# Squares among the gate groups, V's products on two engines and the scan in two halves

## What is computed

```python
h = rms_norm(x, ab_norm_g[i])
proj = h @ ab_w_in[i]
u, q, k, v, gate, a_logit, b_logit = jnp.split(proj, split_points, axis=-1)
a_out = s5_mixer(u, ...)          # 32 groups of 16 channels, 64 complex states
b_out = gated_deltanet(q, k, v, gate, a_logit, b_logit, ...)   # 4 heads, 8 chunks of 64
x = x + jnp.concatenate([a_out, b_out], axis=-1) @ ab_w_out[i]
...
# s5_mixer: s_t = lam_bar * s_(t-1) + b_bar u_t ; y = real(c s_t) + d*u_t ; gelu, then gated
# gated_deltanet: q, k, v through a 4-tap convolution and silu
q = l2_norm(heads(q)) * (GDN_HEAD_DIM ** -0.5)
k = l2_norm(heads(k))
lower = jnp.eye(CHUNK, dtype=F32) + beta[..., :, None] * kk * decay_strict
sol = lax.linalg.triangular_solve(lower, rhs, left_side=True, lower=True, unit_diagonal=True)
```

## Time and profile before

| | us |
|---|---|
| median of 3 runs | 1708.27 (1707.21 to 1708.54) |
| profiled execution, its own time | 1708.71 |
| span of its trace | 1706.9 |
| PE busy | 1648.6 |
| DVE busy | 768.2 |
| ACT busy | 623.9 |
| POOL busy | 253.4 |

### The profile page before, as it was taken

The page is one execution under the profiler, slowest core; times in us unless marked ns, Lnnn a source line. Parts: engine busy times, 40 slices in busy tenths (PEclk is TensorE's granted clock), DMA queues, the critical chain, the costliest instruction groups (busy, mean ns, idle before and its releaser), DMA issues.

```text
span 1706.9 us, 22635 instructions
## 1 busy us (share of the span) xinstructions
PE 1648.6 (97%) x9358; PEld 1343.3 (79%) x9358; DVE 768.2 (45%) x1006; ACT 623.9 (37%) x1010; POOL 253.4 (15%) x315
## 2 busy tenths in 40 slices
PE   5989989999999999999999999999999999999999
PEld 4778788788878788888888887567887788888887
DVE  4658435555444444443225435773453444444222
ACT  6533433344434322221114336564452522222110
POOL 3863034010000211110000003110000011111000
PEclk9999899999999999999999999999999999999999
DMA  6610212034212333332223332322212243333221
GB/s 203 135 50 1 75 52 71 31 123 149 74 49 75 99 98 98 96 97 88 92 95 99 99 123 99 96 78 99 80 45 74 60 113 98 93 93 94 91 98 74
DMA packets 146801, 151.85 MB, mean 89 GB/s; under 512 B 8864, under 2 KB 109344, under 8 KB 146592
## 3 DMA queue, kind: packets, MB, share of 16 engines
q1 hardware_dynamic: 146720, 150.69, 28.9%
HBM read 147.53 MB, written 3.15 MB: 88 GB/s over the span
## 4 chain that ended last, share of the span: by engine, by line
PE 88%; DVE 6%; ACT 4%; issue 2%; POOL 0%; DMA 0%; SPq 0%; DVEq 0%; ACTq 0%; POOLq 0%
PE ps L329 24%; PE ps L331 24%; PE ps L330 24%; PE ps L2070 1%; PE ps L1730 1%; PE ps L425 1%; PE ps L2100 1%; DVE sb L610 1%; PE ps L1707 1%; PE ps L964 1%; DVE w_lo_ab L301 1%; PE ps L2088 1%; ACT sb L1741 1%; ACT sb L2159 1%; PE ps L1242 1%
## 5 line engine op out<-in xcount | busy, mean ns | idle before, releaser
L329 PE MATMUL ps<-h_hi,w_hi 128*128 128x512 f32 x864 | 338.7, 392 | 4.4 <-DVE w_lo L1904 3.9
L330 PE MATMUL ps<-h_lo,w_hi 128*128 128x512 f32 x864 | 337.2, 390 | 0.0
L301 DVE TENSOR_TENSOR w_lo<-raw,w_hi 128x2048 fp32r<-128x2048 f32 x66 | 155.0, 2349 | 341.7 <-ACT w_hi L297 341.7
L297 ACT ACTIVATE w_hi<-raw 128x2048 fp32r<-128x2048 f32 x84 | 160.8, 1915 | 377.1 <-PE ps L331 376.4
L331 PE MATMUL ps<-h_hi,w_lo 128*128 128x512 f32 x704 | 274.4, 390 | 0.0
L329 PEld LDWEIGHTS ps<-h_hi,w_hi 128*128 128x128 f32 x864 | 162.9, 189 | 39.2 <-issue 4.7
L330 PEld LDWEIGHTS ps<-h_lo,w_hi 128*128 128x128 f32 x864 | 162.9, 189 | 33.5
L1904 DVE TENSOR_TENSOR w_lo<-raw,w_hi 128x2048 fp32r<-128x2048 f32 x44 | 138.1, 3139 | 53.5 <-ACT w_hi L1886 53.5
L331 PEld LDWEIGHTS ps<-h_hi,w_lo 128*128 128x128 f32 x704 | 132.5, 188 | 27.8
L1886 ACT ACTIVATE w_hi<-raw 128x2048 fp32r<-128x2048 f32 x44 | 84.3, 1916 | 161.2 <-PE ps L331 161.2
L1914 POOL CAST a_hi<-up 128x512 f32 x44 | 27.0, 613 | 777.2 <-DVE up L1902 777.2
(11 more groups left out here) (378 smaller groups left out, 2697.3 us busy)
## 6 DMA issues: line engine op xcount, KB each, us to landing
raw<-in_f_w_gate SPq DMA_DIRECT2D x44, 512.0 KB, 4.0
raw<-in_f_w_up SPq DMA_DIRECT2D x44, 512.0 KB, 5.2
raw<-in_f_w_down SPq DMA_DIRECT2D x44, 512.0 KB, 4.2
raw<-in_xa_w_kv SPq DMA_DIRECT2D x16, 1024.0 KB, 5.0
raw<-in_c_w_qkv SPq DMA_DIRECT2D x12, 1024.0 KB, 5.1
raw<-in_ab_w_in SPq DMA_DIRECT2D x10, 1024.0 KB, 6.0
raw<-in_xa_w_q SPq DMA_DIRECT2D x8, 1024.0 KB, 5.0
raw<-in_xa_w_out SPq DMA_DIRECT2D x8, 1024.0 KB, 5.0
```

The source lines that it names most:

```text
L297: a.activation(w_hi[:, n % 2, :], raw[n % 2], ACT.Copy).then_inc(sem("w_hi"), 1)
L301: v.tensor_tensor(w_lo(n)[:, n % 2, :], raw[n % 2], w_hi[:, n % 2, :].bitcast(F32), ALU.subtract).then_inc(sem("w_lo"), 1)
L329: pe.matmul(out, a[0], b[0], start=start, stop=False)
L330: pe.matmul(out, a[0], b[1], start=False, stop=False)
```

## The change

Seven things change, all in the first mixer. (1) V's real block goes to GpSimd and its imaginary block to VectorE, each with a scratch of its own. GpSimd's waits only for the tables and for u's copy in DRAM, and lies over u; so u is read back from DRAM (`s5_u_back_sp`, 1 MB) into the place of the output sum. (2) On ScalarE the tables' copies go ahead of silu 7, and TM's copies ahead of piece 8, convolution 9 and silu 8. (3) On VectorE the padded C goes ahead of piece 7 and convolution 7. (4) The 8 squares are put among groups 18 and 19. (5) The scan is done in two halves of 8 group pairs; its banks are arranged so that half 0 frees banks 4 and 5, and `s5_out_pe` works half by half. (6) GpSimd makes the first level's mask of a tile right behind its U_m, and `solve_pe` turns each tile when its own U_m is there. (7) On the last tile ScalarE does the exponential before the copy of q.

```diff
-        V_re, V_im = reg(arena, S5_GP, 8, S5_CH), reg(arena + 2048, S5_GP, 8, S5_CH)
-        v_tmp = reg(base + 10240, S5_GP, 8, S5_CH)
+        V_re, V_im = reg(base + 2048, S5_GP, 8, S5_CH), reg(arena, S5_GP, 8, S5_CH)
+        v_tmp = [reg(base + 10240, S5_GP, 8, S5_CH), reg(arena + 2048, S5_GP, 8, S5_CH)]
...
+                    if k == 4 and mid is not None:
+                        mid()
...
             if f == 0:
-                a.wait_ge(sem("s5_v"), 1)
+                a.wait_ge(sem("s5_vre"), 1)
...
-            g.wait_ge(sem("s5_x"), 2)
+            g.wait_ge(sem("u_out"), 16)
+            g.wait_ge(sem("s5_tab"), 10)
             cr, ci, vr, vi = s5_v_operands()
-            link(g, g.tensor_tensor(V_im, cr, vi, ALU.mult), ch)
-            g.wait_ge(sem("s5_vre"), 1)
-            link(g, g.tensor_tensor(v_tmp, ci, vr, ALU.mult), ch)
-            link(g, g.tensor_tensor(V_im, V_im, v_tmp, ALU.add), "s5_v")
+            link(g, g.tensor_tensor(V_re, cr, vr, ALU.mult), ch)
+            link(g, g.tensor_tensor(v_tmp[0], ci, vi, ALU.mult), ch)
+            link(g, g.tensor_tensor(V_re, V_re, v_tmp[0], ALU.subtract), "s5_vre")
...
+        def s5_u_back_sp(sp):
+            sp.wait_ge(panel_used, AB_PIECES)
+            sp.dma_start(yP, u_dram.rearrange("(f g) c n -> (g c) f n", f=4)).then_inc(sem("u_back"), 16)
...
+            for half in range(2):
+                X_re, X_im = (ps[:, 4 + 2 * half + ri, :].rearrange("p (g c) -> p g c", c=S5_C) for ri in range(2))
+                a, b, c, er, ei, r8 = (w[:, 8 * half:8 * half + 8] for w in (t_a, t_b, t_c, E_re, E_im, R8))
+                link(v, v.tensor_tensor(a, X_re, er, ALU.mult), ch)
...
+                v.memset(a[:, :, 0:1], 0.0).then_inc(sem("s5_carry"), 1)
...
+            for half in range(2):
+                pe.wait_ge(sem("s5_carry"), half + 1)
+                for gp in range(8 * half, 8 * half + 8):
+                    direct(S5_GP + gp)
+                for gp in range(8 * half, 8 * half + 8):
...
         def s5_glu_dve(v):
+            v.wait_ge(sem("u_back"), 16)
...
+                g.wait_ge(sem("g_u"), i + 1)
+                g.tensor_tensor(A_l[:, i], A_T[:, i], bc(ccol("m2"), 1, GH), ALU.mult).then_inc(sem("sv_mask"), 1)
...
         def solve_pe(pe):
-            pe.wait_ge(sem("g_at"), TT)
+            pe.wait_ge(sem("g_tok"), 3 * TT)
             for i in range(TT):
-                pe.wait_ge(sem("g_u"), TT)
+                if i == TT - 1:
+                    pe.wait_ge(sem("g_at"), TT)
+                pe.wait_ge(sem("g_u"), i + 1)
...
-            ab_groups_pe(pe, 15, 19)
-            gdn_squares_pe(pe)
+            ab_groups_pe(pe, 15, 17)
+            gdn_squares_pe(pe, 0, 2)
+            ab_groups_pe(pe, 18, 18, mid=lambda: gdn_squares_pe(pe, 2, 3))
+            gdn_squares_pe(pe, 3, 5)
+            ab_groups_pe(pe, 19, 19, mid=lambda: gdn_squares_pe(pe, 5, 6))
+            gdn_squares_pe(pe, 6, 2 * GH)
...
             for n in range(12):
+                if n == 9:
+                    s5_tm_act(a)
                 if n % 2:
                     pieces_hi(a, *ab_ahead(n + 4))
                 conv_act(a, n)
+                if n == 8:
+                    s5_tables_act(a)
                 if n >= 1:
                     silu_act(a, n - 1)
-                if n == 8:
-                    s5_tables_act(a)
-                if n == 9:
-                    s5_tm_act(a)
...
-            for f in range(4):
-                gate_act(a, f)
-            gdn_squares_act(a, 2, 2 * GH)
+            gate_act(a, 0)
+            gate_act(a, 1)
+            gdn_squares_act(a, 2, 5)
+            gate_act(a, 2)
+            gdn_squares_act(a, 5, 2 * GH)
+            gate_act(a, 3)
...
-                gdn_back_act(a, i)
-                gdn_dec_act(a, i)
...
+                else:
+                    gdn_dec_act(a, i)
+                    gdn_back_act(a, i)
```

More of the change, by code:

```diff
@@ L570, in ab_wait, with ab_groups_pe @@
                 eng.wait_ge(panel_used, where[f"ab{m // 4}_{m % 4 // 2}"] + 1)
-        def ab_groups_pe(pe, first, last):
+        def ab_groups_pe(pe, first, last, mid=None):
             for m in range(first, last + 1):
@@ L754, in s5_v_dve @@
             cr, ci, vr, vi = s5_v_operands()
-            link(v, v.tensor_tensor(V_re, cr, vr, ALU.mult), "dve_step")
-            link(v, v.tensor_tensor(v_tmp, ci, vi, ALU.mult), "dve_step")
-            v.tensor_tensor(V_re, V_re, v_tmp, ALU.subtract).then_inc(sem("s5_vre"), 1)
+            link(v, v.tensor_tensor(V_im, cr, vi, ALU.mult), "dve_step")
+            link(v, v.tensor_tensor(v_tmp[1], ci, vr, ALU.mult), "dve_step")
+            v.tensor_tensor(V_im, V_im, v_tmp[1], ALU.add).then_inc(sem("s5_v"), 1)
         def s5_pad_dve(v):
@@ L887, in s5_out_pe, with direct @@
             pe.wait_ge(sem("gate_s"), 4)
-            for n in (*range(4, S5_GP), *range(4), *range(S5_GP, S5_G)):
+            def direct(n):
                 gp, g2, o = place(n)
+                pe.matmul(o, U2[:, 2 * gp + g2, :], TM[:, 2 * gp + g2, :], start=(gp % 4 == 0), stop=False, skip_group_check=True)
+            for n in (*range(4, S5_GP), *range(4)):
                 if n == 0:
                     pe.wait_ge(sem("g_roots"), after("g_roots", 1))
-                if n == S5_GP:
-                    pe.wait_ge(sem("s5_carry"), 1)
-                pe.matmul(o, U2[:, 2 * gp + g2, :], TM[:, 2 * gp + g2, :], start=(gp % 4 == 0), stop=False, skip_group_check=True)
@@ L895, in s5_out_pe @@
-            pe.wait_ge(sem("s5_carry"), 1)
+                direct(n)
             pe.wait_ge(sem("s5_v"), 1)
[L897 to L907, removed]
+            for half in range(2):
[3 more added lines that the diff above has]
+                for gp in range(8 * half, 8 * half + 8):
+                    for g2 in range(2):
+                        _, _, o = place(gp + S5_GP * g2)
+                        r = slice(g2 * 64, g2 * 64 + 64)
+                        pe.matmul(o, t_b[r, gp, :], V_re[r, gp, :, :].rearrange("p i c -> p (i c)"), start=False, stop=False, skip_group_check=True)
+                    for g2 in range(2):
+                        _, _, o = place(gp + S5_GP * g2)
+                        r = slice(g2 * 64, g2 * 64 + 64)
+                        ins = pe.matmul(o, t_a[r, gp, :], V_im[r, gp, :, :].rearrange("p i c -> p (i c)"), start=False, stop=True, skip_group_check=True)
+                    if gp % 4 == 3:
+                        ins.then_inc(sem("s5_y"), 1)
@@ L1074, in gdn_squares_act, with gdn_squares_pe @@
                 a.activation(sq_T[:, n % 2, :], qkvT[:, n, :], ACT.Square).then_inc(sem("g_sq"), 1)
-        def gdn_squares_pe(pe):
-            for n in range(2 * GH):
+        def gdn_squares_pe(pe, first, last):
+            for n in range(first, last):
                 pe.wait_ge(sem("g_sq"), n + 1)
@@ L2353, in _ @@
             load_pieces(sp, "ab2_1", "ab4_1")
+            s5_u_back_sp(sp)
             load_panel(sp, "glu")
@@ L2561, in _ @@
             for n in range(12):
+                if n == 7:
+                    s5_pad_dve(v)
                 if n % 2:
@@ L2573, in _ @@
                     s5_g_dve(v, G_AT.index(n))
-                if n == 7:
-                    s5_pad_dve(v)
                 if n == 10:
```

45 lines of the change are left out of this document (20 added, 25 removed).

## The result

The changed kernel takes 1690.69 us (median of 4 runs, 1688.55 to 1691.43) against 1707.74 for the kernel before beside it: a ratio of 0.990, 95% interval 0.9885 to 0.9916. That is 17 us less. The forecast was 1693.6, range 1689 to 1700. The profiled execution is the fastest of the four, 1688.55, with a span of 1686.8, and that of the kernel before, 1708.71, was a little slower than its median. So the two traces compared here differ by 20.1, three more than the medians.

The account below looks back on a forecast made before the run. TensorE, busy 97% of the span, was taken as the bound, with waits and half-clock stretches to remove. Terms summed to -14.7 us from the profiled 1708.71, giving 1694.0, or 1693.6 as median; range 1689 to 1700.

Parts of the forecast that it names:

- Bound: Whole kernel: TensorE busy 97% of the span, so only its idle time, work or half-clock stretches can shorten it.
- Tables, TM, group 14: First mixer: earlier copies save 6.4 us in the tables and 2.2 in TM; full clock saves 1.3 in group 14.
- Squares and direct products: Squares put among the groups and direct products behind them, both at full clock: 1.5 and 1.4 us less.
- the eight switches: TensorE's changes between groups and squares: 0.4 us added, between 0 and 1.
- Scan in halves and reading u back: VectorE's scan chain ends at 168.3, slack 1.5, cost 0 to +2 us; u lands before it is wanted, cost 0.
- V on GpSimd: Three GpSimd products end near 127, with collisions 133; cost 0, with 3.6 us of cover in the worst case.
- Solve: Start of the solve: three of four turns fall into the wait for GpSimd, exponential goes first; 2.3 us less.
- A: Rival: transposes of the tables and TM don't hold the clock; 1697 to 1701 us, chance 0.08.
- B: Rival: squares drag the clock down among the groups, two to four falls; 1696.5 to 1700 us, chance 0.09.
- C: Rival: VectorE's chain ends late, TensorE waits for the squares' copy; +1 to +3 us, chance 0.05 beyond the forecast.
- D: Rival: the gain is given back at unseen places, bank or piece waits; within 3.4 us of before, chance 0.04.
- E: Rival: slower, all from first squares to last small products at half clock; 1709 us or more, chance 0.04.

Follow-up runs that it names:

- finer waits: The changed kernel with two TensorE waits split: tables' transposes wait only for the groups of G they read, the first turn bank by bank; 1692.96 us, ratio 0.9916.
- changed kernel's second profile: The changed kernel itself, nothing altered, timed again beside later kernels: median 1690.42 us (1688.4 to 1695.7); the profiled run was its slowest.

## Why the prediction was right, step by step

**Bound.** Right: waits on the other engines' order and the clock falls behind them. Undoing either of two lines of order, one on ScalarE and one on VectorE, brings a wait and a fall back.

**Tables, TM, group 14.** 6.4, 2.2 and 1.3 forecast, 6.6, 2.5 and 1.4 measured. The padded copies took 1.72, not 3.48 as in the earlier trace rows. Most single copies take 0.13 to 0.18 in both kernels. One of the eight took 1.04 in the changed kernel (from 102.56, beside an operation of GpSimd that ran to 103.55), and two took 1.26 and 1.04 before, each also done within 0.1 of the end of a GpSimd operation. That the copies stood behind GpSimd is inferred from these three places; no run isolates it.

**Squares and direct products.** 1.1 and 1.4 forecast, 1.4 and 1.4 measured; the eight switches cost 0.2 at most together, not 0.4 (34.7 less five groups of 5.47 is 7.4, for 64 passes of 0.113). The run with the squares in one piece shows that squares in one long run bring the clock down without a wait, as the earlier trace rows suggested.

**Scan in halves and reading u back.** Cost 0 each, as forecast. For the scan this is shown by the kernel with the whole scan; the chain's 22.8 was forecast as 22.7. No wait of TensorE for u's copy appears.

**V on GpSimd.** The time was right, the cover wrong. I named group 16 as the one to wait for the low part of piece 8, with 3.6 of cover. The low part did collide (4.37 instead of 2.29), and what it pushed was not group 16 but the work behind it: VectorE's convolutions, then ScalarE's silu 11, two squares and gate 0, with 0.4 to spare. It costs nothing in the changed kernel and ate what the finer waits saved ahead of it. My sentence that ScalarE's squares are not late by my schedule was true by luck.

**Solve.** Forecast 2.3. Undone it costs 2.7 by the medians and 2.9 by the stage. From the kernel before to the changed one the stage gave 2.9 too, 0.3 of it the tail of the fall at 198.7 (line 964 took 14.31, line 976 takes 14.00). The fall behind the wait for GpSimd the prediction left out: line 1242's 64 products took 3.22 before, line 1255's take 2.69.

**The sum.** The forecast was 2.9 above the median, and the sum of 14.7 is 5.4 short of the 20.1 between the two profiles. Of these, 1.1 lie in the turn, 0.3 in its tail and 2.6 behind the solve's first product: falls of the clock at 198.7, 241 and 1093 before and none there after. The prediction left such falls out of the sum and put 1.6 either way in the range. The other 1.4 are small excesses of the terms and the 0.2 of the earlier start. The fall at 241 stood behind the wait for GpSimd that the change shortens. The other two are chance as far as these profiles show: behind the wait of 1.4 to 1.5 ahead of the turn a fall comes in five of the ten profiles that have the wait, and near 1073 to 1096 in ten of all 14. The changed kernel's second profile has both, in a run of 1695.7. So about 3 of the 20.1 are the luck of the two profiled runs, about as much as the medians are closer.

**The rivals.** A fell: the transposes of the tables and of TM, alone on TensorE for 3.8 us (102.02 to 105.81) and 3.4 us (118.53 to 121.94), ran at 1.00, and so did what followed. The Trainium skill's sentence in TensorE: Matmul & The Clock Gate, "Part 4: PE-mode transpose", that transposes don't count as busy, is not what this trace shows; already spoke against it. B fell for the changed kernel. In the kernels with finer waits the clock did fall at the interleaved squares, with a wait of 1.4 or 0.4 ahead of them. That is one profile each and doesn't part the wait from the squares. C fell with a slack of 1.1. D and E fell: nothing ahead of the solve was given back, and in the changed kernel no stretch of squares among the groups ran at half clock.

## What to carry to other kernels

Look at the granted clock of every stage whose busy share is 100%: here 11.4 of 20.1 us were busy time, most of it products at half clock, so that a wait of 4.0 us cost 6.6. Some of these falls stood behind waits, one behind a long run of squares, and some came and went between runs of the same kernel; take more than one profile before crediting a change with them. When work is moved to an idle engine, look for the engine whose operations it makes longer (here VectorE, 4.37 for 2.29), and follow that one down to the next wait of TensorE, not just to the first reader. Undo each part of a combined change alone before crediting it: of these, the halved scan chain was worth nothing, and two reorderings of the tables overlapped in what they gave.

## What the runs showed of the hardware

- TensorE lost half its clock with no wait at all: with the squares in one piece it was busy in all of 160.80 to 164.20, with products of 128x128 weights and one streamed column, and stood at 0.50 for the 10.2 us behind that.
- A wait of 0.4 us with 1.9 us of such products behind it was followed by a fall in one profile, and the same products, 8 or 16 passes at a time among the groups, without a wait by none in the eight profiles that have them so.
- A fall at the turn, 3.4 us at 0.50, cost 1.3 to 1.6 us in the five profiles that have it, the one behind the long run of squares, 10.2 us at 0.50, 4.7.
- A scan on VectorE with both inputs in SBUF took 5.40 beside a GpSimd operation (one case) and 1.22 alone. So the scan waited as the products with two SBUF inputs do. The Trainium skill gives this as the rule for VectorE operations with two SBUF inputs in SBUF — State Buffer, "Who interferes with whom". The trace agrees.
